# Hybrid decoder step on one core: the values' projection put first, the head norms' small loads put later, four late places for the last decode values, and the first gate product moved to behind unit 57

## What is computed

```python
h = rms_norm(x, norm1_w) @ w_in              # 3*512 + 4*512 + 2*1024 columns
q, k, v, q_hg, f, i, g, gate_a, gate_b = split(h)
q, k = rms_norm over each head of q and k
o_sb = sb_prompt(q, k, v)                    # 512 prompt tokens, 8 heads of 64
o_sb = sb_decode(q, k, v, k_past, v_past)    # 8 sequences x 4096 cached rows, through page_table
o_hg, state = hgrn2_chunked(...)             # recurrent mixer
y_b = rms_norm(o_hg, hg_norm_w) * silu(g)
merged = sigmoid(gate_a) * (o_sb @ w_branch_a) + sigmoid(gate_b) * (y_b @ w_branch_b)
x = x + merged @ w_out
x = x + hier_moe(rms_norm(x, norm2_w))       # 32 experts, top 2 inside the top group
```

## Time and profile before

| | |
|---|---|
| median of 3 runs | 1463.33 us (1458.17 to 1467.6) |
| the profiled execution, its own time | 1469.55 us |
| its span | 1467.8 us |
| TensorE busy | 1305.1 us, 89% of the span |
| VectorE, ScalarE, GpSimd busy | 400.2, 354.3, 87.7 us |
| moved by DMA | 395.96 MB, mean 270 GB/s |
| granted TensorE clock, mean | 0.938 of full speed |
| the chain that ended last, by engine | TensorE 78%, DMA 6%, issue 6%, SyncE's queue 6% |

### The profile page before, as it was taken

One profiled execution on the slowest core, in us unless ns is written; L12 is line 12 of the kernel. 1 busy time (PEld: TensorE's weight loads), 2 busy tenths in 40 slices (PEclk: granted clock), 3 DMA queues, 4 the chain that ended last, 5 costly groups with the idle time before them and its releaser, 6 DMA issues.

```text
span 1467.8 us, 22495 instructions
## 1 busy us (share of the span) xinstructions
PE 1305.1 (89%) x8892; PEld 785.7 (54%) x8892; DVE 400.2 (27%) x745; ACT 354.3 (24%) x575; POOL 87.7 (6%) x146
## 2 busy tenths in 40 slices
PE   6999999989999999876999999979988788888782
PEld 5857545756767776544888875533333233333231
DVE  2012465634434335531010023431101100101103
ACT  2023334434445445742000002201000000000000
POOL 3000000020000002000000000001110100010000
PEclk9999999989999989999999999979999989999887
DMA  6114201067999989999941132189999999999985
GB/s 233 58 58 138 86 1 56 30 185 270 379 340 353 342 312 378 387 385 324 335 155 58 58 131 117 49 328 425 425 425 427 425 427 425 426 427 424 427 367 195
DMA packets 119641, 395.96 MB, mean 270 GB/s; under 512 B 17075, under 2 KB 25284, under 8 KB 107250
## 3 DMA queue, kind: packets, MB, share of 16 engines
q1 hardware_dynamic: 109506, 380.41, 66.8%
q0 software_dynamic: 5984, 11.18, 2.2%
q10 hardware_dynamic: 4048, 2.93, 0.6%
HBM read 386.06 MB, written 16.27 MB: 274 GB/s over the span
## 4 chain that ended last, share of the span: by engine, by line
PE 78%; DMA 6%; issue 6%; SPq 6%; DVE 2%; ACT 1%; ACTq 0%; POOLq 0%; DVEq 0%
PE ps L1152 16%; PE ps L672 8%; PE ps L975 8%; PE ps L1175 7%; PE ps L798 6%; PE ps L675 6%; PE ps L978 4%; PE ps L1039 4%; PE ps L809 3%; PE ps L831 3%; DMA arena<-in_w_gate_exp 2%; SPq L391 2%; SPq L383 2%; DMA arena<-in_cache_k 2%; PE ps L722 1%
## 5 line engine op out<-in xcount | busy, mean ns | idle before, releaser
L1152 PE MATMUL ps<-arena 128*64 128x512 f32 x512 | 255.6, 658 | 68.4 <-issue 66.9
L1153 PE MATMUL ps<-arena 128*64 128x512 f32 x512 | 256.1, 659 | 0.0
L1152 PEld LDWEIGHTS ps<-arena 128*64 128x64 f32 x512 | 74.7, 152 | 214.9 <-issue 212.8
L798 PE MATMUL ps<-ident,arena 128*128 128x128 f32 x1024 | 149.7, 292 | 25.3 <-DMA arena<-in_cache_k 23.2
L798 PEld LDWEIGHTS ps<-ident,arena 128*128 128x128 f32 x1024 | 118.0, 148 | 97.0 <-issue 67.1
L1383 ACT ACTIVATE arena<-ps 128x512 f32<-128x512 f32 x192 | 109.0, 596 | 174.5 <-PE ps L798 174.2
L975 PE MATMUL ps<-mixers,arena 128*128 128x272 f32 x512 | 120.4, 396 | 7.4 <-DMA arena<-in_w_in 7.4
L672 PE MATMUL ps<-mixers,arena 128*128 128x272 f32 x512 | 121.0, 397 | 0.5 <-DVE mixers L1533 0.5
L975 PEld LDWEIGHTS ps<-mixers,arena 128*128 128x128 f32 x512 | 98.0, 192 | 28.2 <-DMA arena<-in_w_in 7.7
L672 PEld LDWEIGHTS ps<-mixers,arena 128*128 128x128 f32 x512 | 97.8, 192 | 21.2 <-DVE mixers L1533 0.6
L1794 DVE COPY arena<-ps 128x512 f32<-128x512 f32 x64 | 44.2, 690 | 177.5 <-PE ps L798 177.5
(11 more groups left out here) (343 smaller groups left out, 1348.3 us busy)
## 6 DMA issues: line engine op xcount, KB each, us to landing
arena<-in_cache_k SPq DMA_DIRECT2D x256, 256.0 KB, 5.3
arena<-in_w_gate_exp SPq DMA_DIRECT2D x32, 2048.0 KB, 32.5
arena<-in_w_up_exp SPq DMA_DIRECT2D x32, 2048.0 KB, 37.0
arena<-in_cache_v SPq DMA_DIRECT2D x252, 256.0 KB, 5.5
arena<-in_w_down_exp SPq DMA_DIRECT2D x22, 2048.0 KB, 37.8
mixers<-in_w_down_exp SPq DMA_DIRECT2D x10, 2048.0 KB, 37.6
arena<-in_w_in SPq DMA_DIRECT2D x7, 2048.0 KB, 10.3
arena<-in_w_in SPq DMA_DIRECT2D x8, 1024.0 KB, 13.5
```

The costliest lines, as they stand in the source:

```text
L798: last = turn(ps[:, turned_at(n, j), P * c:P * c + P], keys_of(n)[:, j, P * c:P * c + P], ident[:, :])
L1152: mm(ps[0:BLK, 1 + u, :], own, wgv[w][:, k, :], start=k == 0, stop=k == KD - 1)
L1153: last = mm(ps[BLK:P, 1 + u, :], own, wuv[w][:, k, :], start=k == 0, stop=k == KD - 1)
```

## The change

Head. The chunk of the values becomes chunk 0 (`IN_AT` gives each chunk's columns). SyncE issues two token tiles, then that chunk's weights, then the other tiles. TensorE turns tiles 0 and 1, then does the values' job of tile 0, turns tile 2, does the job of tile 1, and so on; the turns use banks 0 to 3 in place of 4 to 7, and a values' job waits only for its own tile's `hT`. ScalarE loads its table first, then issues `norm1_w`, makes the five roots and only then issues the seven other small loads. Jobs 0 to 15 now run in a row (`AHEAD`), `head_sums` of q stand behind job 10, those of k behind job 13, and `FILL` spreads the other 120 steps.

Decode's end. Units 60 and 61 get places of their own (34304, where the sample states were, and 36352), units 62 and 63 the ring places of units 57 and 58. So the loads of units 60 and 61 wait for no sum, that of unit 62 for unit 57's and that of unit 63 for unit 58's. `gate_loads(0)` is issued three turns earlier, ahead of the load of unit 58, and `branch_product(0, 0)` stands right behind the values of unit 57.

The semaphores of the token tiles' three loads (`x_loaded_i`, `y_loaded_i`) are joined in `tile_loaded_i`, with the counts raised.

```diff
+        late_values = {UNITS - 4: carve(34304, GP, 512), UNITS - 3: carve(36352, GP, 512),
+                       UNITS - 2: vring[:, (UNITS - 7) % 3], UNITS - 1: vring[:, (UNITS - 6) % 3]}
...
-        CHUNKS = [("cols", qT), ("cols", kT), ("rows", vtok), ("cols", hqT), ("rows", ftok), ("rows", itok),
+        CHUNKS = [("rows", vtok), ("cols", qT), ("cols", kT), ("cols", hqT), ("rows", ftok), ("rows", itok),
                   ("cols", gT)]
...
-        FILL = [(0, 13), (4, 12), (4, 9), (3, 19), (4, 10), (4, 18), (4, 9), (4, 11)]
+        IN_AT = [512 * c for c in (2, 0, 1, 3, 4, 5, 6)]
+
+        AHEAD = QKV + 3
+        FILL = [(0, 12), (3, 12), (3, 9), (9, 12), (3, 9), (3, 18), (3, 9), (3, 12)]
...
-            for i in range(NT):
-                sp.dma_start(xt[0:ROWS[i], i, :], x_tok[i]).then_inc(S(f"x_loaded_{i}"), 16)
+            for i in range(2):
+                sp.dma_start(xt[0:ROWS[i], i, :], x_tok[i]).then_inc(S(f"tile_loaded_{i}"), 16)
+            sp.dma_start(wring[:, 0], w_in[:, :, IN_AT[0]:IN_AT[0] + 512]).then_inc(S("w_in_0"), 16)
+            for i in range(2, NT):
+                sp.dma_start(xt[0:ROWS[i], i, :], x_tok[i]).then_inc(S(f"tile_loaded_{i}"), 16)
...
-                if n >= 3:
+                if n == UNITS - 4:
+                    sp.wait_ge(S("states_stored"), 16 * (2 + 2 * NB))
+                elif n >= UNITS - 2:
+                    sp.wait_ge(S("values_summed"), n - 4)
+                elif 3 <= n < UNITS - 4:
                     sp.wait_ge(S("values_summed"), n - 2)
...
-                if n == UNITS + 4:
+                if n == UNITS + 1:
                     sp.wait_ge(S("yb"), 1)
                     gate_loads(0)
...
+                if c == 0:
+                    pe.wait_ge(S("hT"), 2 * j + 2)
...
-            for n in range(8):
+            turn_x(0)
+            for i in range(1, NT):
+                turn_x(i)
+                project(i - 1)
+            for n in range(NT - 1, QKV - 2):
                 project(n)
             head_sums(0)
-            for n in range(8, QKV):
+            for n in range(QKV - 2, QKV + 1):
                 project(n)
             head_sums(1)
-            for n in range(QKV, QKV + 2):
+            for n in range(QKV + 1, AHEAD):
                 project(n)
...
             unit_scores(UNITS - 1)
-            for n in range(UNITS - LAG, UNITS - PER_SET):
-                unit_values(n)
+            unit_values(UNITS - LAG)
+            branch_product(0, 0)
+            unit_values(UNITS - 6)
+            unit_values(UNITS - 5)
             turn_weights(NSET * NGRP - 1)
-            branch_product(0, 0)
+            pe.wait_ge(S("set_softplus"), 4 * NSET * NGRP - 3)
+            branch_product(0, 1)
             unit_values(UNITS - 4)
             unit_values(UNITS - 3)
-            pe.wait_ge(S("set_softplus"), 4 * NSET * NGRP - 3)
-            branch_product(0, 1)
             unit_values(UNITS - 2)
             unit_values(UNITS - 1)
             turn_values(1)
...
+            nc.scalar.preload_act_table_set("natural_log_exp_and_others")
             load(w1c[:, :], a["norm1_w"][0].rearrange("(p k) -> p k", k=KD), "w1_loaded")
...
-            nc.scalar.preload_act_table_set("natural_log_exp_and_others")
```

More of the change, by code:

```diff
@@ L282, in filled @@
             return own
-        assert sum(sum(f) for f in FILL) == KD * (len(JOBS) - QKV - 2)
+        assert sum(sum(f) for f in FILL) == KD * (len(JOBS) - AHEAD)
         TURN, ZB, VB, WB = 0, 2, 6, 7
@@ L1247, in _ @@
                 fn(rstd[0:r, i:i + 1], rstd[0:r, i:i + 1], ACT.Exp, scale=-0.5).then_inc(S("row_roots"), 1)
+            for j, name in enumerate(("q_norm_w", "k_norm_w", "hg_norm_w")):
+                for e in range(2):
+                    load(qkg[64 * e:64 * e + 64, j:j + 1], a[name][0].rearrange("(p o) -> p o", o=1), "small_loaded")
+            load(bias8[:, :], a["sb_bias"].to_broadcast([P, H]), "small_loaded")
             def projection_out(n):
@@ L1947, in placed @@
                 dve.sem_inc(S("codes"), 1)
[L1949 removed]
+            dve.wait_ge(S("tile_loaded_4"), 32)
             samples_added()
```

52 lines of the change are left out of this document (27 added, 25 removed).

## The result

| | before | after |
|---|---|---|
| median of 20 runs | 1464.09 us (1458.17 to 1472.49) | 1449.22 us (1442.94 to 1458.68) |
| ratio of the times | | 0.991, 95% interval 0.989 to 0.9929 |
| the profiled execution, its own time | 1469.55 us | 1444.44 us |
| its span | 1467.8 us | 1442.7 us |
| granted TensorE clock, mean | 0.938 | 0.95 |

The ratio is a gain of 0.009 x 1464.09 = 13.2 us (its interval is 10.4 to 16.1), the medians differ by 14.9; 13.6 us were predicted. The two profiled executions differ by 25.1 us, which is more than the kernels do. So the first question is which part of those 25.1 us belongs to the change.

A forecast was written before the change was run, and what follows sets the result against it. It took the decode's first part as bound by TensorE, its second by transfers, the experts by their weights. Terms 4.3 + 1.6 + 1.2 + 6.5 = 13.6 us took the median 1463.33 to 1449.7 us; range 1443 to about 1459.

The forecast's parts named there:

- The first square: Head, ScalarE: it starts when tile 0 lands, at 4.5 us; TensorE is through with tiles 0 and 1 at 10.6.
- step (b): Head: the first chunk's weights follow tile 1 and land last, at 11.3 us, where the first job starts.
- the hole: Head, 5 to 11 us: loads at only 244 GB/s, laid to the small loads; otherwise 1.9 us of gain are gone.
- step (d): Head: the fall of TensorE's clock to 0.54 from 20.4 to 23.8 us does not come; 1.6 us more gain.
- step (c): Head: transposes of tiles 2 to 4 stand between jobs without waiting, 3 x 1.16 = 3.5 us.
- The attention: Prompt attention: head 3's wait of 1.25 us for ScalarE's copy goes; gain 1.2 us, bounds 0 and 1.3.
- The decode's end: End of the decode: earlier gate weights and new order make it end at 704.8 instead of 711.28; gain 6.5 us.
- Carrying: Behind the decode: what is won in front of 711.5 us should move the whole rest forward.
- R3: Decode's end or experts: the change does not carry; only the head's few us or nothing remain, 1456 to 1463 us; chance 0.10.
- R1: Head: the rate hole stays, or the clock falls once all the same; gain 10.1 to 12, 1451 to 1453 us; chance 0.25.
- R2: First gate product: the clock is spared there too; gain 15.2 or more, 1448 us or less; chance 0.17.
- R4: Decode's first part: slower, as TensorE meets the clock's half level more often; each 0.01 costs 2.6 us; chance 0.04.

The follow-up runs named there:

- small_first: The changed kernel with the seven small loads issued right behind that of `norm1_w`, ahead of the roots; median 1453.97 us, ratio 0.9942.
- after_ctl: The changed kernel as it is, run again beside other runs on one chip; median 1452.76 us, ratio 0.9936.
- after_again: The changed kernel once more, beside a repeat of early_warm on one chip; median 1450.4 us, ratio 0.9904.
- head_only: The changed kernel with the ring of three, gate weights and order of the decode's end as before; median 1458.22 us, ratio 0.9971.
- fill_wait: The changed kernel with head 3's first slot in `FILL` as before, three steps for nine, and 18 in its second; one run, 1456.83 us.
- warm: The changed kernel with 24 idle transposes ahead of the first token tile and 32 between unit 57's values and the gate product; median 1453.41 us.
- early_gate: The changed kernel with gate weights issued at unit 57's keys and the first gate product in pieces in units 58 to 63; median 1445.58 us.
- early_warm: The kernel of early_gate with 24 idle transposes ahead of the first token tile; medians 1444.98 and 1443.68 us in two sets.

## Why the prediction was right

The predicted 13.6 us stand against 13.2. Point by point:

- **The first square** starts at 4.79 us (4.5 predicted), and TensorE is through with tiles 0 and 1 at 7.43 + 3.65 = 11.1 (10.6).
- **The first weights, step (b)**, landed at 1.7 + 10.2 = 11.9 us, not at 11.3, because tile 1 came at 6.0 and not 5.8 and the stretch ran at 372 GB/s, not 380. The weights end last, as said, and the job starts at 12.0 to 12.4. The small loads as the cause of the hole are shown by small_first, with 1.3 us; the rest of the hole is open.
- **The clock in the head, step (d)**, was counted at 1.6 us and is true in five of eight profiles: 7.13 us for the first job in after_ctl and after_again among them, 9.03 and 9.02 in after and head_only. The first scores come 5.7 and 5.5 us earlier in the first two, 3.9 and 3.7 in the others; predicted were 4.3 + 1.6 = 5.9. The pause before the job was 0.9 to 1.8 us instead of 0.7. The rule cited from "TensorE: Matmul & The Clock Gate" of the Trainium skill, that activity has to release the clock, is what the 9.03 us agree with, and it is not enough to say which of the two comes.
- **The transposes between the jobs, step (c)**, were counted at 1.16 us each and took 0.9 to 1.0 (the first from 20.88 to 21.77 us), 0.7 us less in all.
- **The attention**: 1.4 to 1.5 us, 1.2 predicted. The size holds. The mechanism is half shown: the wait of the earlier trace rows is gone, but fill_wait, which was to bring it back, brought another one (0.94 us for VectorE). What made the wait of before is read from its trace and not shown by a run.
- **The decode's end**: 4.8 to 5.2 us, 6.5 predicted, and this is the term that was mis-sized. From unit 57's values to the turn of the sums before took 711.28 - 675.17 = 36.1 us, predicted were 29.6, and after took 687.34 - 656.35 = 31.0. The wait was 4.85 (4.7 predicted), the part behind the product 14.8 (15.1). The product took 10.25 us instead of 8.95: I had left before's loss to the clock in, 1.6 us, and behind the new pause it is 10.25 - 7.6 = 2.7. warm shows that it is the pause: with the pause filled the product takes 7.60.
- **Carrying**: 253.4 us to the experts in both, the experts 503.2 and 502.1. Rival R3 fell.
- **The rivals**: of R1 its second half, a clock that falls once in the head, is true in three of eight profiles; its first half fell. R2 fell for the changed kernel (the clock was lost in the gate product in all of its profiles) and was made true by warm, in the product though not in the time (1453.41 us, R2 has 1448 or less). R4 fell; the decode's clock was rather higher than lower.
- **What the number owes to luck**: the terms measured in their places sum to 10.6 (after) to 11.9 us (after_ctl), some 2 to 3 us less than predicted, and the clock elsewhere gives back about that much, which was no step of mine. The other two sets of the changed kernel have ratios of 0.9936 and 0.9904 (9.3 and 14.1 us of 1461.3 and 1464.65), and at one clock the gain is 8.0 us, so that 13.2 came so close to 13.6 is partly luck.

## What to carry to other kernels

Before the stages of two profiles are compared, compare their granted clocks: here one kernel's decode took 364.6 or 374.9 us, and the means of before's four sets agree within 0.5 us when brought to one clock, where the raw means lie 2.2 apart and the runs of one set 15. Where a product is moved to fill a pause, its weights' place in the queue and the places for what is queued behind it have to move with it; with either of them left behind, the end was no shorter than before the change. And the pause in front of the first gate product cost twice, its own length and the slow start behind it (2.7 us); filling such pauses with pieces of the next product gained 5.2 (early_gate) and 6.4 us (early_warm) at one clock, although the piece's weights then push other loads back by about as long as they take themselves (5.6 us).

## What the hardware showed that was not expected

Seven small loads on ScalarE's queue (six of them of 64 single numbers) took SyncE's large ones from 372 to 285 GB/s over 6 us. Idle transposes kept the clock for the gate product, behind a pause of 1.71 us; in the head, at the start of the launch, they did not decide: behind pauses of 2.68, 2.71 and 2.37 us the first job was whole once (7.13 us) and slow twice (8.83 and 8.73), and without them it was whole in five of eight profiles. What decides there is open. And one and the same kernel's decode runs at a mean granted clock of 0.95 or 0.98, 10 us apart, with nothing in the program to tell the two apart.
